# A decoder trunk on one core: the expert rows are put back by two rounded matmuls, and the gate enters at the add

## The chip, the cores and the metric

The kernel runs on one core of a Trainium2 chip. The metric is the device time of one execution in microseconds, here the median of several runs. Five engines matter: TensorE (PE in the rows, with PEld for its weight loads), VectorE (DVE), ScalarE (ACT), GpSimd (POOL) and SyncE (SP), which only starts transfers here. Each engine takes its instructions in order; semaphores order the engines against each other.

## The reference, cut to what matters

The program is a two-layer decoder trunk for 256 tokens of width 1024. The second layer's channel mixer is a mixture of eight experts, each a SwiGLU of width 3584, and every token goes to its best two:

```
top_logit, top_e = lax.top_k(xt @ w_router, 2)
gate = jax.nn.softmax(top_logit, axis=-1)
g, u = jnp.split(xblk @ w_in[e], 2, axis=-1)      # rows of expert e, 128 at a time
yb = (jax.nn.silu(g) * u) @ w_out[e]
out = zeros.at[buf_tok].add(yb * buf_w[:, None])   # buf_w: the gate of each row
h = layer_norm(ALPHA * h + out, ln_g, ln_b)
```

Everything is float32. What this document is about is the line with `add`: the output rows of an expert are multiplied by the gate and added to their tokens.

## The kernel before

The first 554 us or so compute both attention layers, the dense mixer and the router. The rest is a loop of at least eight steps (`steps` is read from the data; it is eight here), one step for each expert, on 128 rows at a time.

Matrix products use *rounded* operands (type float32r, in the names ending in `h` and `l`). A float32 matrix is split in a high part, rounded by ACT, and a low part, the difference, made by DVE. A product is then three rounded matmuls (`product`, L806 to L808): high by high, low by high, high by low. The weights of an expert come as 42 items of 1 MB. For every item SP starts a transfer to one of 11 slots, ACT rounds it into `wh` (L750, 128x2048), DVE writes the difference into `wl` (L1593), and PE does 12 matmuls of 512 columns with it. `wh` and `wl` have three places (`SPLITS`), so ACT may round item k+3 only once PE has used item k (semaphore `used`), DVE follows ACT (`rounded`), and PE follows DVE (`split`). In the body of the loop ACT and DVE run k from 3 to 44, which means that the last three passes (42 to 44) prepare items 0 to 2 of the next expert, and the body begins with item 3.

The order of the other work is written out in a table, `EXPERT_WORK`: before the item k that stands there, ACT and DVE do the activation (`act`), the high and low parts of the turned activation (`turn`), the building of the 0/1 matrices (`build`, `rows`), the taking of the expert's output (`y`, at k = 44, so right before item 2 of the next expert) and the adding back (`back`, at k = 6 and 8).

The rows of one expert go back like this. `put` (128 tokens x 128 slots, twice) holds at [token, slot] the gate if the token has that slot, else 0. PE turns it into `putT`. The output lies in two banks of PSUM, 6 and 7; ACT copies one half into `ysb` (L781) and DVE the other (L1578), both as plain float32. During the next step, after items 3 and 5, PE multiplies `putT` by `ysb` (`scatter`, L1113): four plain float32 matmuls of 512 columns, two after item 3 and two after item 5. DVE adds each result to `pre` (`add_back`, L1550). After the last step four more scatters, the adds and the norm follow, and the output is stored. In the first step `ysb` and `putT` are zeros.

Of the kernel before, what the change touches and what calls it, by code (L numbers as in the profile page):

```python
# [14 lines left out]
P = 128  # L15
# [113 lines left out]
def decoder_kernel(nc, x, positions, w_in_a, w_out_a, cmp_pos, cmp_w1, cmp_w2, w_kv_shared, w_q_b, w_out_b,  # L129
                   sinks_b, ln_g, ln_b, dense_w_in, dense_w_out, moe_router, moe_w_in, moe_w_out, out):  # L130
    ctx = ExitStack()
    with ctx:
# [115 lines left out]
        eactTl = room(3072, 2, 4, P, of=arena_r)  # L248
        act = room(4096, 2, 512)
        esilu = room(5120, 2, 512)  # L250
        ysb = room(6144, D)
        pick = room(7168, NT, P)
        put = room(7424, NT, P)
        putT = room(7680, NT, P)
        slot_at = [ring[:, s, :] for s in range(RING)] + [room(8192, UNIT), room(10240, UNIT), slot9[:, :], slot10[:, :]]

        bank = [ctx.enter_context(nc.psum_tensor(f"bank{i}", [P, 512], F32)) for i in range(8)]
# [65 lines left out]
        e_rows = sem("e_rows")  # L323
        e_rows_high = sem("e_rows_high")
        e_rows_low = sem("e_rows_low")
        e_y_a = sem("e_y_a")
        e_y_v = sem("e_y_v")
        e_back = sem("e_back")
        e_added = sem("e_added")
        done = sem("done")  # L330
# [145 lines left out]
        @block.gpsimd  # L476
        def _(pool):
            n = [0]

            def step(ins):  # L480
                n[0] += 1
                ins.then_inc(consts_step, 1)
                pool.wait_ge(consts_step, n[0])

            step(pool.memset(ident[:, :], 0.0))
            step(pool.affine_select(out=ident[:, :], in_=ident[:, :], compare_op=ALU.not_equal, fill=1.0, base=0,
                                    pattern=[[-1, P]], channel_multiplier=1))
            pool.sem_inc(ident_ready, 1)
            step(pool.tensor_copy(identb[:, :], ident[:, :]))
            for j in range(ROT // 2):  # L490
                step(pool.memset(freq[:, j:j + 1], float(ROPE_THETA ** (-2.0 * j / ROT))))
            step(pool.memset(causal[:, :, :], 0.0))
            step(pool.memset(window[:, :, :], 0.0))
            for m in (causal, window):
                step(pool.affine_select(out=m[:, 1, :], in_=m[:, 1, :], compare_op=ALU.is_ge, fill=NEG, base=0,
                                        pattern=[[-1, P]], channel_multiplier=1))
            step(pool.affine_select(out=window[:, 0, :], in_=window[:, 0, :], compare_op=ALU.is_ge, fill=NEG, base=-1,
                                    pattern=[[1, P]], channel_multiplier=-1))
            step(pool.memset(cmpmask[:, :, :, :], NEG))
            for tt in range(NT):  # L500
                for g in range(4):
                    part = cmpmask[:, tt, g, 16 * g:16 * g + 16]
                    step(pool.memset(part, 0.0))
                    step(pool.affine_select(out=part, in_=part, compare_op=ALU.is_ge, fill=NEG,
                                            base=P * tt - (2 * CMP_STRIDE - 1), pattern=[[-CMP_STRIDE, 16]],
                                            channel_multiplier=1))
            step(pool.memset(seen[:, :], 1.0))
            step(pool.affine_select(out=seen[:, 0:1], in_=seen[:, 0:1], compare_op=ALU.is_ge, fill=0.0,
                                    base=-(2 * CMP_STRIDE - 1), pattern=[[0, 1]], channel_multiplier=1))
            step(pool.memset(onesb[:, :], 1.0))  # L510
            step(pool.affine_select(out=earlier[:, :], in_=onesb[:, :], compare_op=ALU.is_ge, fill=0.0, base=-1,
                                    pattern=[[1, P]], channel_multiplier=-1))
            step(pool.iota(slots[:, :], [[1, P]], base=0, channel_multiplier=0, allow_small_or_imprecise_dtypes=True))
            step(pool.iota(order[:, :, :], [[0, NT], [-1, NE]], base=NE, channel_multiplier=0,
                           allow_small_or_imprecise_dtypes=True))
            step(pool.memset(cmp_in[:, :, :, :], 0.0))
            pool.memset(slotx[:, :, 16:17], -1.0).then_inc(consts, 1)
            pool.memset(gatex[:, :, 16:17], 0.0).then_inc(consts, 1)

            pool.wait_ge(h_ready, 12)  # L520
            pool.tensor_scalar(pre[:, :, :], h[:, :, :], ALPHA, None, ALU.mult).then_inc(e_added, 1)
# [3 lines left out]
        def _(act_e):  # L525
# [225 lines left out]

            norm_part(2, T_H3)
            split_weights(N_FIRST + SPLITS)
            act_e.sem_inc(e_y_a, 1)
            act_e.wait_ge(gap_ready, 1)
            act_e.activation(top[:, 5, :, :], top[:, 4, :, :], ACT.Exp).then_inc(gap_exp, 1)

# [8 lines left out]
            def expert_step(i):  # L766

                for k in range(SPLITS, PER_EXPERT + SPLITS):
                    for what, f in EXPERT_WORK.get(k, ()):
                        if what == "act":  # L770
                            expert_used(act_e, i, EXPERT.index(("g", f, 1)))
                            act_e.wait_ge(e_act, i * FT + max(f - 1, 0) + 1)
                            act_e.activation(esilu[:, f % 2, :], bank[2 * (f % 2)][:, :], ACT.Silu).then_inc(e_silu, 1)
                        elif what == "turn":
                            act_e.wait_ge(e_turned, i * FT + f + 2)
                            act_e.activation(eactTh[:, f % 2, :, :],  # L776
                                             bank[4 + f % 2][:, :].rearrange("p (c n) -> p c n", c=4), ACT.Copy)\
                                 .then_inc(e_high, 1)
                        elif what == "y":
                            expert_used(act_e, i, PER_EXPERT - 1)  # L780
                            act_e.activation(ysb[:, 0:512], bank[6][:, :], ACT.Copy).then_inc(e_y_a, 1)  # L781
                        elif what == "rows":
                            take_rows(i + 2)
                    split_expert(i, k)
# [10 lines left out]
        def _(pe):  # L795
# [307 lines left out]
            def scatter(v, n, last=False):  # L1103

                if n == 0:
                    pe.wait_ge(e_putT_moved, v)
                    pe.wait_ge(e_y_a, v)
                if n == 1:
                    pe.wait_ge(e_y_v, v)
                tt, half = n // 2, n % 2  # L1110
                if n >= 2 and not last:
                    pe.wait_ge(e_added, 4 * v + n - 4)
                pe.matmul(bank[n if last and n >= 2 else 4 + n % 2][:, :], putT[:, tt, :], ysb[:, 512 * half:512 * half + 512],  # L1113
                          start=True, stop=True).then_inc(e_back, 1)


            pe.sem_inc(e_turned, 1)
# [56 lines left out]
        def _(dve):  # L1174
# [354 lines left out]
            step(dve.tensor_tensor(g2, egap, g1, ALU.mult))  # L1529
            step(dve.tensor_tensor(gw, pick1, g1.to_broadcast(wide), ALU.mult))  # L1530
            step(dve.tensor_tensor(tmp, pick2, g2.to_broadcast(wide), ALU.mult))
            dve.tensor_tensor(gatex[:, :, 0:NE], gw, tmp, ALU.add)
            step(dve.tensor_tensor(gatex[:, :, NE:2 * NE], gw, tmp, ALU.add))


            def take_rows(value):
# [3 lines left out]
                    dve.tensor_tensor(xgTl[there], bank[2 + q][:, :].rearrange("p (c n) -> p c n", c=4),  # L1540
                                      xgTh[there].bitcast(F32), ALU.subtract).then_inc(e_rows_low, 1)

            def add_back(v, parts, last=False):

                dve.wait_ge(e_added, 4 * v - 3)
                for n in parts:
                    tt, half = n // 2, n % 2
                    dve.wait_ge(e_back, 4 * v + n - 3)
                    cols = slice(512 * half, 512 * half + 512)
                    dve.tensor_tensor(pre[:, tt, cols], pre[:, tt, cols],  # L1550
                                      bank[n if last and n >= 2 else 4 + n % 2][:, :], ALU.add)\
                       .then_inc(e_added, 1)


            dve.memset(putT, 0.0).then_inc(e_putT_moved, 1)
            dve.memset(ysb, 0.0).then_inc(e_y_v, 1)
            dve.sem_inc(e_act, 1)
            take_rows(1)
            dve.wait_ge(plan_ready, 1)
# [1 line left out]
            with dve.Fori(0, steps) as i:  # L1561
                for k in range(SPLITS, PER_EXPERT + SPLITS):
                    for what, f in EXPERT_WORK.get(k, ()):
# [8 lines left out]
                            dve.tensor_tensor(eactTl[:, f % 2, :, :], bank[4 + f % 2][:, :].rearrange("p (c n) -> p c n", c=4),  # L1572
                                              eactTh[:, f % 2, :, :].bitcast(F32), ALU.subtract).then_inc(e_low, 1)
                        elif what == "back":
                            add_back(i + 1, range(2 * f, 2 * f + 2))
                        elif what == "y":
                            expert_used(dve, i, PER_EXPERT - 1)
                            dve.tensor_copy(ysb[:, 512:1024], bank[7][:, :]).then_inc(e_y_v, 1)  # L1578
                        elif what == "build":
                            build_pick(ds(i + 1, 1), i + 1)  # L1580
                            dve.wait_ge(e_putT, i + 1)
                            for tt in range(NT):
                                ins = dve.tensor_scalar(put[:, tt, :], slots[:, :], slotx[:, tt, ds(i, 1)],
                                                        gatex[:, tt, ds(i, 1)], ALU.is_equal, ALU.mult)
                            ins.then_inc(e_put, 1)
                        else:
                            dve.wait_ge(e_putT, i + 2)
# [8 lines left out]

            dve.wait_ge(ln_landed, 32 * 4)
            for tt in range(NT):
                add_back(steps + 1, range(2 * tt, 2 * tt + 2), last=True)
                dve.wait_ge(e_added, 4 * steps + 3 + 2 * tt)  # L1600
                for half in range(2):
                    chained(dve.bn_stats(stats[:, tt, half, :], pre[:, tt, 512 * half:512 * half + 512]))
                center(tt)
# [25 lines left out]
```

## Time and profile before

| what | value |
|---|---|
| median of 3 runs | 1574.53 us (1573.82 to 1575.28) |
| span of the profiled execution | 1573.7 us, 20472 instructions |
| PE busy | 1512.1 us (96%) |
| DVE busy | 1230.3 us (78%) |
| ACT busy | 982.5 us (62%) |
| POOL busy | 15.2 us (1%) |
| chain that ended last | PE 91%, DVE 5%, ACT 2%, issue 1%, DMA 1% |
| read from memory | 424.14 MB, 270 GB/s over the span |

The profiled execution has no time of its own besides its span; the median of the runs lies 0.8 us above that span. The busy times overlap, so they don't add up. Most of the span belongs to the expert loop, from about 554 us to 1555 us. The last row of the page on the chain says which engine the end of the kernel waited for, step by step, and it counts more than the busy shares.

### The profile page before, as it was taken

How to read it: one execution, taken by the hardware profiler on the slowest of the kernel's cores; microseconds unless marked ns; L12 is line 12 of the kernel's file. 1: busy time of each engine (PE TensorE's matmuls, PEld its weight loads, DVE VectorE, ACT ScalarE, POOL GpSimd, SP SyncE). 2: the span in 40 equal slices, each digit the busy share in tenths (PEclk: the TensorE clock that was granted, in tenths of full speed). 3: DMA queues.
4: the chain of work that ended last, by engine and by line, in shares of the span. 5: the costliest groups of instructions: out<-in, count | busy, mean ns of one | idle time of the engine just before them, and what ended most of it. 6: DMA issues, size and time to landing. Idle time of an engine off the chain costs nothing.

```text
span 1573.7 us, 20472 instructions
## 1 busy us (share of the span) xinstructions
PE 1512.1 (96%) x7467; PEld 1244.6 (79%) x7467; DVE 1230.3 (78%) x1143; ACT 982.5 (62%) x964; POOL 15.2 (1%) x47
## 2 busy tenths in 40 slices
PE   6989989999889799999999999999999999999996
PEld 5876679998776588878888888887887887887884
DVE  5667865454666779889888988988988988988988
ACT  4554534443344367777767777777767777776774
POOL 2000000000000100000000000000000000000000
PEclk9978999999998899999999999999999999999998
DMA  9660026555560489999999999999999999999990
GB/s 333 161 214 1 1 70 199 187 186 188 160 189 1 176 292 346 360 352 334 362 366 356 341 353 354 353 341 359 344 344 367 345 370 334 345 376 347 341 346 27
DMA packets 200922, 425.78 MB, mean 271 GB/s; under 512 B 10384, under 2 KB 42160, under 8 KB 200880
## 3 DMA queue, kind: packets, MB, share of 16 engines
q1 hardware_dynamic: 196864, 419.65, 74.5%
q10 hardware_dynamic: 4016, 5.56, 1.1%
q8 instruction: 27, 0.44, 0.1%
q14 instruction: 15, 0.12, 0.0%
HBM read 424.14 MB, written 1.05 MB: 270 GB/s over the span
## 4 chain that ended last, share of the span: by engine, by line
PE 91%; DVE 5%; ACT 2%; issue 1%; DMA 1%; ACTq 0%; DVEq 0%
PE bank L806 26%; PE bank L808 26%; PE bank L807 26%; PE bank L962 3%; PE bank L823 2%; PE bank L1098 2%; PE bank L1113 2%; PE bank L1159 2%; PE bank L985 1%; PE bank L980 1%; ACT wh L555 1%; DVE wl L1190 1%; DVE h L1435 1%; DVE pre L1426 1%; DVE stats L1419 1%
## 5 line engine op out<-in xcount | busy, mean ns | idle before, releaser
L806 PE MATMUL bank<-wh,arena_r 128*128 128x512 f32 x1432 | 570.5, 398 | 0.0
L1593 DVE TENSOR_TENSOR wl<-ring,wh 128x2048 fp32r<-128x2048 f32 x224 | 512.1, 2291 | 64.9 <-ACT wh L750 64.3
L808 PE MATMUL bank<-wl,arena_r 128*128 128x512 f32 x1432 | 558.5, 390 | 0.0
L807 PE MATMUL bank<-wh,arena_r 128*128 128x512 f32 x1432 | 557.6, 389 | 0.0
L750 ACT ACTIVATE wh<-ring 128x2048 fp32r<-128x2048 f32 x224 | 428.8, 1917 | 93.5 <-PE bank L808 93.4
L806 PEld LDWEIGHTS bank<-wh,arena_r 128*128 128x128 f32 x1432 | 268.9, 188 | 59.3 <-issue 3.8
L807 PEld LDWEIGHTS bank<-wh,arena_r 128*128 128x128 f32 x1432 | 269.1, 188 | 57.7 <-issue 3.8
L808 PEld LDWEIGHTS bank<-wl,arena_r 128*128 128x128 f32 x1432 | 268.8, 188 | 57.4
L1190 DVE TENSOR_TENSOR wl<-ring,wh 128x2048 fp32r<-128x2048 f32 (+1 forms) x64 | 144.7, 2264 | 112.6 <-ACT wh L555 112.6
L555 ACT ACTIVATE wh<-ring 128x2048 fp32r<-128x2048 f32 (+1 forms) x64 | 120.8, 1893 | 128.8 <-PE bank L808 124.4
L1593 DVE TENSOR_TENSOR wl<-arena,wh 128x2048 fp32r<-128x2048 f32 x64 | 146.7, 2292 | 27.7 <-ACT wh L750 27.7
L750 ACT ACTIVATE wh<-arena 128x2048 fp32r<-128x2048 f32 x64 | 122.7, 1917 | 48.8 <-PE bank L808 48.8
L1593 DVE TENSOR_TENSOR wl<-slot,wh 128x2048 fp32r<-128x2048 f32 x48 | 110.0, 2291 | 37.7 <-ACT wh L750 37.7
L750 ACT ACTIVATE wh<-slot 128x2048 fp32r<-128x2048 f32 x48 | 92.1, 1918 | 53.2 <-PE bank L808 53.2
L806 PE MATMUL bank<-hTh,wh 128*128 128x256 f32 x352 | 100.4, 285 | 1.4 <-DVE hTl L1202 1.4
L807 PE MATMUL bank<-hTh,wl 128*128 128x256 f32 x352 | 100.3, 285 | 0.0
L808 PE MATMUL bank<-hTl,wh 128*128 128x256 f32 x352 | 100.2, 285 | 0.0
L806 PE MATMUL bank<-wh,hTh 128*128 128x512 f32 (+2 forms) x208 | 82.6, 397 | 8.3 <-DVE wl L1190 6.5
L689 ACT ACTIVATE arena<-bank,nb 128x128 f32<-128x128 f32 (+1 forms) x128 | 50.7, 406 | 61.4 <-DVE nb L1379 43.7
L808 PE MATMUL bank<-wl,hTh 128*128 128x512 f32 (+2 forms) x208 | 80.0, 385 | 0.0
L807 PE MATMUL bank<-wh,hTl 128*128 128x512 f32 (+2 forms) x208 | 80.0, 385 | 0.0
L776 ACT ACTIVATE arena_r<-bank 128x512 fp32r<-128x512 f32 x56 | 33.5, 599 | 61.8 <-PE bank L1159 61.8
(214 smaller groups left out, 1403.4 us busy)
## 6 DMA issues: line engine op xcount, KB each, us to landing
ring<-in_moe_w_in_dram SPq DMA_DIRECT2D x171, 1024.0 KB
ring<-in_moe_w_out_dram SPq DMA_DIRECT2D x56, 1024.0 KB
arena<-in_moe_w_out_dram SPq DMA_DIRECT2D x40, 1024.0 KB, 5.5
slot<-in_moe_w_in_dram SPq DMA_DIRECT2D x32, 1024.0 KB, 5.0
arena<-in_moe_w_in_dram SPq DMA_DIRECT2D x24, 1024.0 KB, 6.2
ring<-in_dense_w_in_dram SPq DMA_DIRECT2D x22, 1024.0 KB
slot<-in_moe_w_out_dram SPq DMA_DIRECT2D x16, 1024.0 KB, 6.4
ring<-in_dense_w_out_dram SPq DMA_DIRECT2D x11, 1024.0 KB
```

Of the source, the lines that this page charges most:

```text
L555: act_e.activation(wh[:, n % SPLITS, 0:size], slot_of(n)[:, 0:size], ACT.Copy).then_inc(rounded, 1)
L689: ins = act_e.activation(ex[:, i % (lag + 1), k * w:k * w + w], bank[i % 4][:, k * w:k * w + w], ACT.Exp, bias=nb[:, i % 4, k:k + 1], scal ...
L750: act_e.activation(wh[:, n % SPLITS, :], slot_at[SLOT[k % PER_EXPERT]], ACT.Copy).then_inc(rounded, 1)
L776: act_e.activation(eactTh[:, f % 2, :, :], bank[4 + f % 2][:, :].rearrange("p (c n) -> p c n", c=4), ACT.Copy)\
L806: pe.matmul(out_, lh, rh, start=start, stop=False, skip_group_check=True)
L807: pe.matmul(out_, ll, rh, start=False, stop=False, skip_group_check=True)
L808: return pe.matmul(out_, lh, rl, start=False, stop=stop, skip_group_check=True)
L823: ins = pe.transpose(b[:, at:at + rows], src, ident[0:rows, 0:rows])
L962: ins = pe.matmul(sc[:, k * w:k * w + w], q[half, 4 * pb + h0 + k, tt * P:tt * P + P], keys, start=False, stop=(k == nh - 1), skip_group_c ...
L1098: ins = pe.matmul(bank[2 + c // 4][:, (c % 4) * P:(c % 4) * P + P], h[:, tt, c * P:c * P + P], pick[:, tt, :], start=(tt == 0), stop=(tt = ...
L1190: dve.tensor_tensor(wl[:, n % SPLITS, 0:size], slot_of(n)[:, 0:size], wh[:, n % SPLITS, 0:size].bitcast(F32), ALU.subtract).then_inc(split, 1)
L1593: dve.tensor_tensor(wl[:, n % SPLITS, :], slot_at[SLOT[k % PER_EXPERT]], wh[:, n % SPLITS, :].bitcast(F32), ALU.subtract).then_inc(split, 1)
```

## The change

The plain float32 scatter becomes two rounded ones. `putT` is now rounded (float32r) and holds only 0 and 1, since `put` is built without the gate; the output of an expert is kept as a high part `yh`, rounded by ACT from both banks, and a low part `yl`, the difference, made by DVE in two halves. Each scatter is `putT` by `yh` plus `putT` by `yl`, into the same bank. The gate is multiplied in by DVE at the add: `scalar_tensor_tensor` computes bank times gate plus `pre` in one instruction, with the gate as one value per token from `gatex`. `gatex` is shifted by one column, because the first adding back (of zeros) has no expert yet. `yl` has no room of its own: its halves lie in `act[:, 1]` and `esilu[:, 1]`, and so ACT waits for the last scatter before it writes `esilu[:, 1]`.

```
-        ysb = room(6144, D)
+        yh = room(6144, D, of=arena_r)
+        yl = [room(at, 512, of=arena_r) for at in (4096 + 512, 5120 + 512)]
-        putT = room(7680, NT, P)
+        putT = room(7680, NT, P, of=arena_r)
...
                         if what == "act":
                             expert_used(act_e, i, EXPERT.index(("g", f, 1)))
+                            if f == 1:
+                                act_e.wait_ge(e_back, 4 * i + 4)
...
-                            act_e.activation(ysb[:, 0:512], bank[6][:, :], ACT.Copy).then_inc(e_y_a, 1)
+                            for half in range(2):
+                                act_e.activation(yh[:, 512 * half:512 * half + 512], bank[6 + half][:, :], ACT.Copy)\
+                                     .then_inc(e_y_high, 1)
...
                 if n == 0:
                     pe.wait_ge(e_putT_moved, v)
-                    pe.wait_ge(e_y_a, v)
-                if n == 1:
-                    pe.wait_ge(e_y_v, v)
+                if n < 2:
+                    pe.wait_ge(e_y_low, 2 * v + n - 1)
...
-                pe.matmul(bank[n if last and n >= 2 else 4 + n % 2][:, :], putT[:, tt, :], ysb[:, 512 * half:512 * half + 512],
-                          start=True, stop=True).then_inc(e_back, 1)
+                there = bank[n if last and n >= 2 else 4 + n % 2][:, :]
+                pe.matmul(there, putT[:, tt, :], yh[:, 512 * half:512 * half + 512], start=True, stop=False)
+                pe.matmul(there, putT[:, tt, :], yl[half], start=False, stop=True).then_inc(e_back, 1)
...
-                    dve.tensor_tensor(pre[:, tt, cols], pre[:, tt, cols],
-                                      bank[n if last and n >= 2 else 4 + n % 2][:, :], ALU.add)\
-                       .then_inc(e_added, 1)
-            dve.memset(putT, 0.0).then_inc(e_putT_moved, 1)
-            dve.memset(ysb, 0.0).then_inc(e_y_v, 1)
+                    dve.scalar_tensor_tensor(out=pre[:, tt, cols], in0=bank[n if last and n >= 2 else 4 + n % 2][:, :],
+                                             scalar=gatex[:, tt, ds(turn, 1)], in1=pre[:, tt, cols],
+                                             op0=ALU.mult, op1=ALU.add).then_inc(e_added, 1)
+            dve.memset(putT.bitcast(F32), 0.0).then_inc(e_putT_moved, 1)
+            dve.memset(yh.bitcast(F32), 0.0)
+            for half in range(2):
+                dve.memset(yl[half].bitcast(F32), 0.0).then_inc(e_y_low, 1)
...
-                            dve.tensor_copy(ysb[:, 512:1024], bank[7][:, :]).then_inc(e_y_v, 1)
+                            for half in range(2):
+                                dve.wait_ge(e_y_high, 2 * i + half + 1)
+                                dve.tensor_tensor(yl[half], bank[6 + half][:, :],
+                                                  yh[:, 512 * half:512 * half + 512].bitcast(F32), ALU.subtract)\
+                                   .then_inc(e_y_low, 1)
...
                                 ins = dve.tensor_scalar(put[:, tt, :], slots[:, :], slotx[:, tt, ds(i, 1)],
-                                                        gatex[:, tt, ds(i, 1)], ALU.is_equal, ALU.mult)
+                                                        None, ALU.is_equal)
```

ACT at the end of the loop body, where the expert's output is taken; the row before `COMPARE_AND_BRANCH` and its register row is item 2 of the next expert. Before the change:

```order
L781 ACTIVATE arena_61<-bank6 128x512
L394 REGISTER_ALU
L750 ACTIVATE wh_50<-ring_49 128x2048
L789 REGISTER_ALU
L789 COMPARE_AND_BRANCH
```

and after it:

```order
L784 ACTIVATE arena_r_62<-bank6 128x512
L784 ACTIVATE arena_r_62<-bank7 128x512
L395 REGISTER_ALU
L751 ACTIVATE wh_50<-ring_49 128x2048
L793 REGISTER_ALU
L793 COMPARE_AND_BRANCH
```

ACT now has two copies out of the banks ahead of item 2, where it had one.

DVE at the same place, first before the change and then after it (`wl` is the low part of an item, `bank6` and `bank7` hold the expert's output):

```order
L1578 COPY arena_61<-bank7 128x512
L1592 REGISTER_ALU
L1593 TENSOR_TENSOR wl_51<-ring_49,wh_50 128x2048
```

```order
L1585 ISA
L1586 TENSOR_TENSOR arena_r_62<-bank6,arena_r_62 128x512
L1585 REGISTER_ALU
L1586 TENSOR_TENSOR arena_r_62<-bank7,arena_r_62 128x512
L1602 REGISTER_ALU
L1603 TENSOR_TENSOR wl_51<-ring_49,wh_50 128x2048
```

One copy has become two subtractions, still ahead of item 2's low part.

## Rows read from the trace of the kernel before

**Rows 1.** Busy time by stretch: us, PE, PEld, DVE, ACT, POOL, PEclk, DMA, GB/s

```profile
543.00:678.90 135.90, 130.86 (x614) 108.37 (x615) 113.26 (x102) 90.53 (x62) 0.00 (x0) 0.97 0.91 330
678.90:804.10 125.20, 125.20 (x576) 102.59 (x575) 109.28 (x69) 91.39 (x61) 0.00 (x0) 1.00 0.96 352
```

**Rows 2.** Waits of the loop, 553.7 to 1555 us: total, times, longest

```profile
PEld bank L806 <- DVE wl L1593: 2.2, 7, 0.3
```

**Rows 3.** Waits of SP's queue in the loop, from 560 us

```profile
SPq L457 <- DVE wl L1593: 787.6, 318, 15.7
```

**Rows 4.** The chain that ended last, around one scatter: start, us, what

```profile
690.09 1.72 PE bank L1113 x4
691.80 0.23 PE bank L806
692.03 0.23 PE bank L807
```

**Rows 5.** Groups by line, shapes apart: busy us, mean ns, idle before

```profile
L806 PE MATMUL bank<-wh,arena_r 128*128 128x512 f32 x1432 | 570.5, 398 | 0.0
L1113 PE MATMUL bank<-arena 128*128 128x512 f32 x72 | 34.0, 594 | 1.1 <-ACT arena L781 0.8 <-DVE arena L1578 0.3
L1550 DVE TENSOR_TENSOR pre<-pre,bank 128x512 f32<-128x512 f32 x36 | 23.0, 679 | 0.0
L1435 DVE SCALAR_TENSOR_TENSOR h<-pre,std,lnp 128x512 f32<-128x512 f32 x16 | 11.3, 750 | 0.3
```

**Rows 6.** PE's timeline after the turn of an expert: start, us, what

```profile
686.75 0.39 PE L808 MATMUL bank<-wl,arena_r 128*128 128x512 f32 x1
687.03 0.50 PE L806 MATMUL bank<-wh,arena_r 128*128 128x512 f32 x1
687.37 0.40 PE L807 MATMUL bank<-wh,arena_r 128*128 128x512 f32 x1
...
689.70 0.39 PE L808 MATMUL bank<-wl,arena_r 128*128 128x512 f32 x1
...
691.87 0.40 PE L807 MATMUL bank<-wh,arena_r 128*128 128x512 f32 x1
```

**Rows 7.** ACT's timeline at the turn of an expert

```profile
679.02 0.60 ACT L781 ACTIVATE arena<-bank 128x512 f32<-128x512 f32 x1 [0.80 <-PE bank L808]
679.51 1.91 ACT L750 ACTIVATE wh<-ring 128x2048 fp32r<-128x2048 f32 x1
681.44 1.28 ACT L750 ACT_TABLE_LOAD   x1
682.73 3.72 ACT L750 ACTIVATE wh<-ring 128x2048 fp32r<-128x2048 f32 x2
```

**Rows 8.** DVE's timeline at the turn of an expert

```profile
680.46 0.68 DVE L1578 COPY arena<-bank 128x512 f32<-128x512 f32 x1
681.45 2.29 DVE L1593 TENSOR_TENSOR wl<-ring,wh 128x2048 fp32r<-128x2048 f32 x1 [0.31 <-ACT wh L750]
684.68 6.74 DVE L1593 TENSOR_TENSOR wl<-ring,wh 128x2048 fp32r<-128x2048 f32 x3 [0.94 <-ACT wh L750]
...
693.13 2.28 DVE L1593 TENSOR_TENSOR wl<-ring,wh 128x2048 fp32r<-128x2048 f32 x1
```

**Rows 9.** Timeline of all engines after the last expert

```profile
1555.20 0.60 ACT L781 ACTIVATE arena<-bank 128x512 f32<-128x512 f32 x1 [0.80 <-PE bank L808]
1555.70 1.90 ACT L750 ACTIVATE wh<-ring 128x2048 fp32r<-128x2048 f32 x1
...
1557.38 2.84 PE L1113 MATMUL bank<-arena 128*128 128x512 f32 x6 [0.34 <-DVE arena L1578]
...
1557.63 2.29 DVE L1593 TENSOR_TENSOR wl<-ring,wh 128x2048 fp32r<-128x2048 f32 x1 [0.30 <-ACT wh L750]
...
1559.84 1.28 DVE L1550 TENSOR_TENSOR pre<-pre,bank 128x512 f32<-128x512 f32 x2
```

**Rows 10.** Timeline of all engines ahead of the first expert

```profile
550.97 0.91 DVE L1556 MEMSET arena<- 128x1024 f32 x1 [0.16 <-issue]
...
552.83 0.69 DVE L1540 TENSOR_TENSOR arena_r<-bank,arena_r 128x512 fp32r<-128x512 f32 x1 [0.94 <-ACT arena_r L762]
...
553.75 0.49 PE L806 MATMUL bank<-wh,arena_r 128*128 128x512 f32 x1
```

More of the change, by code:

```diff
@@ L325, in decoder_kernel @@
         e_rows_low = sem("e_rows_low")
-        e_y_a = sem("e_y_a")
-        e_y_v = sem("e_y_v")
+        e_y_high = sem("e_y_high")
+        e_y_low = sem("e_y_low")
         e_back = sem("e_back")
@@ L517, in _ @@
             pool.memset(slotx[:, :, 16:17], -1.0).then_inc(consts, 1)
-            pool.memset(gatex[:, :, 16:17], 0.0).then_inc(consts, 1)
+            pool.memset(gatex[:, :, 0:1], 0.0).then_inc(consts, 1)
             pool.wait_ge(h_ready, 12)
@@ L753, in _ @@
             split_weights(N_FIRST + SPLITS)
-            act_e.sem_inc(e_y_a, 1)
             act_e.wait_ge(gap_ready, 1)
@@ L1531, in _ @@
             step(dve.tensor_tensor(tmp, pick2, g2.to_broadcast(wide), ALU.mult))
-            dve.tensor_tensor(gatex[:, :, 0:NE], gw, tmp, ALU.add)
-            step(dve.tensor_tensor(gatex[:, :, NE:2 * NE], gw, tmp, ALU.add))
+            dve.tensor_tensor(gatex[:, :, 1:1 + NE], gw, tmp, ALU.add)
+            step(dve.tensor_tensor(gatex[:, :, 1 + NE:1 + 2 * NE], gw, tmp, ALU.add))
             def take_rows(value):
@@ L1541, in take_rows, with add_back @@
                                       xgTh[there].bitcast(F32), ALU.subtract).then_inc(e_rows_low, 1)
-            def add_back(v, parts, last=False):
+            def add_back(v, turn, parts, last=False):
                 dve.wait_ge(e_added, 4 * v - 3)
@@ L1574, in _ @@
                         elif what == "back":
-                            add_back(i + 1, range(2 * f, 2 * f + 2))
+                            add_back(i + 1, i, range(2 * f, 2 * f + 2))
                         elif what == "y":
                             expert_used(dve, i, PER_EXPERT - 1)
-                            dve.tensor_copy(ysb[:, 512:1024], bank[7][:, :]).then_inc(e_y_v, 1)
+                            for half in range(2):
[3 more added lines that the diff above has]
+                                   .then_inc(e_y_low, 1)
                         elif what == "build":
@@ L1598, in _ @@
             for tt in range(NT):
-                add_back(steps + 1, range(2 * tt, 2 * tt + 2), last=True)
+                add_back(steps + 1, steps, range(2 * tt, 2 * tt + 2), last=True)
                 dve.wait_ge(e_added, 4 * steps + 3 + 2 * tt)
```

## The prediction

> **What bounds the kernel now.** I read the busy times by stretch first, since the shares of the whole span mix stages. One step of the expert loop takes 125.20 us, PE is busy for all of it, DVE for 109.28 us and ACT for 91.39 us [rows 1]. The waits of the loop say the same: PE waits seven times for a low part of the weights, 2.2 us in all, once at each turn from one expert to the next [rows 2]. The loads are not the bound, although the DMA engines are busy for 0.96 of a step: their queue stands 787.6 us waiting for free slots, and slots are freed by DVE [rows 3]. So in the loop the end is set by PE's own work, and DVE and ACT feed it with a few microseconds to spare, least at the turn of an expert. Last come the timelines of PE, ACT and DVE around one turn [rows 6 to 8]; the reader should see who is late there.
>
> **The scatter (gain).** A plain float32 matmul leaves two records: 72 records for 36 matmuls [rows 5]. The recorded length, 594 ns, is not what PE pays, because records overlap. In the chain a pair of scatters (four records) takes 1.72 us, so one scatter 0.86 us, while a rounded matmul of the same shape takes one place of 0.23 us [rows 4]. The pair becomes four rounded matmuls of 128x128 by 512 columns, the form of L806, which stands 1432 times in the trace: 4 x 0.23 = 0.92 us. The gain is 0.80 us a pair. The starts agree: from the L808 ahead of the pair to the second matmul behind it are 691.87 - 689.70 = 2.17 us [rows 6]; six places of 0.23 are 1.38, and the gain is 0.79. There are 16 pairs in the loop (two in each of eight steps, the zeros of the first step included), all where PE bounds: 16 x 0.80 = 12.8 us. The other four scatters stand after the loop and are looked at below.
>
> On this price the trace and the Trainium skill don't quite agree. In the trace a plain float32 scatter costs 0.86 us against 0.23 us for a rounded one, 3.8 places [rows 4]. The Trainium skill, FP8 and Floating Point Precision, section "TensorE Precision Notes", says that true FP32 takes four passes through the array. By that rule, with each pass at the 0.23 us of a rounded matmul, a pair would cost 1.84 us and its replacement 0.92, which makes 16 x 0.92 = 14.7 us instead of 12.8, and the time 1.9 us lower; I go by the row.
>
> **ACT at the turn (loss).** ACT copies bank 6 at 679.02, rounds item 2 from 679.51, loads a table, and rounds item 3 from 682.73 [rows 7]. These follow each other without a gap, so ACT itself is what is late. DVE's low part of item 3 starts at 684.68, right when ACT is done (it sat idle for 0.94 us before that), and takes about 2.29 us [rows 8], and PE's item 3 starts at 687.03, where it should have followed the L808 at 686.75 by 0.23 [rows 6]. So PE is already late there by this chain, and what is put into it shows in full. The change puts a second copy of 128x512 ahead of item 2. Two ACT instructions of this kind follow each other by 0.49 us (679.02 to 679.51) [rows 7]. Item 3 is ready 0.49 us later at each of the 7 turns inside the loop: 3.4 us. Item 2 moves as well: its low part starts at 681.94 instead of 681.45 [rows 8] and ends at 684.23. PE begins item 2 at 686.75 - 11 x 0.227 = 684.26 (twelve matmuls, the last at 686.75), so this is just in time or 0.1 us late; such a slip is contained in the 0.49, since PE waits for item 3 anyway.
>
> Is DVE in time for this? It takes the low halves at 680.46 and about 681.1, each 0.68 us as the copy does, and ACT's copies land at 679.6 and 680.1. DVE is free at 681.7, before the 681.94 at which ACT hands over item 2. So the second subtraction is covered by the wait for ACT (0.31 us before item 2 plus the 0.49 added) [rows 8]. Without that cover it would cost 0.6 us a turn. PE's wait for `yl` is over at 681.8, eight microseconds ahead of the scatter.
>
> **Items 4 to 8 (nothing).** The shorter pairs take 0.8 us of time away from ACT and DVE, twice. DVE makes the low parts of items 3 to 5 one behind the other, 2.2 us apart [rows 8]; PE starts item 3 at 687.52 and takes 2.8 us for an item and 0.92 for a pair. So the low part of item 4 ends at 689.7 against 691.2 when PE wants it, item 5 at 691.9 against 693.9, item 6, behind the activation and two adds, at about 696.0 (before: 693.13 + 2.28 = 695.4 [rows 8]) against 697.6. The spare time is 1.5 us or more at each, so no new wait.
>
> **The add (nothing in the loop).** The form with a scalar per token takes 750 ns where both tensors are in SBUF, the plain add 679 ns [rows 5]; the new one lies between 0 and 0.07 us above the old. In the loop DVE has 16 us a step to spare [rows 1]. I take 0.07.
>
> **The tail (loss).** After the last expert the four scatters are not what is waited for: PE begins the last three at 1557.38 and is done with them well before DVE, which first makes a low part that nobody needs (1557.63, when ACT hands it over) and adds from 1559.84 [rows 9]. ACT's extra 0.49 us moves that hand-over; the scatters' gain is worth nothing here. Four adds on the way to the end cost up to 4 x 0.07 = 0.3 us. Loss: 0.8 us.
>
> **The rest (nothing).** The zeroing grows by two halves of 512 columns, about as much as the 0.91 us of the present 1024 [rows 10]. The DVE instruction behind it starts at 552.83 after 0.94 us of idling, and PE starts at 553.75: nothing, at most 0.1 us. ACT's new wait before `esilu[:, 1]` stands two items behind item 8, the last scatter ahead of item 6: it is over before. Building `put` without the gate saves DVE a little where it has room.
>
> **The sum.** 12.8 - 3.4 - 0.8 = 8.6 us. Against the profiled span, 1573.7 - 8.6 = 1565.1 us. The median of the runs lies 0.8 us above that span, so I forecast 1565.9 us.
>
> **Rivals.**
> *The turn hides the copy.* If ACT's table load or the item behind it absorbs the second copy (a shorter gap between copies, or DVE catching up), 0 instead of 3.4 us is lost: 12.0 us gained, 1562.5 us; with the price of the four passes 1560.6 us. Against it: ACT shows no gap between 679.02 and the end of item 4 [rows 7]. Chance 0.14.
> *The feed becomes the bound behind the scatters.* Were item 6 or 7 late, the second pair's 0.80 us would be lost in eight steps: 6.4 us less, 1572.3 us. For it speaks that everything hangs on three places of `wh`; against it the spare 1.5 us. Chance 0.08, with the smaller losses between.
> *Slower: the rounded scatter is not cheap.* It would be so if the matmul on `putT`, written by DVE's copy, ran at the pace of the plain form, or if two matmuls that accumulate into one bank cost more than two apart. The change costs 3.4 + 0.8 = 4.2 us elsewhere, 0.26 us a pair; from (1.72 - 0.26) / 4 = 0.365 us for each rounded matmul on, the kernel is slower. At 0.43 (a record of the plain form) it is 1574.5 + 4.2 = 1578.7 us. The 1432 matmuls at 0.23 [rows 4, 5] speak against it. Chance 0.03.
> *PE's granted clock falls.* It is 1.00 in the loop and 0.97 in the stretch that holds the loop's start [rows 1]. At 0.99 a thousand microseconds of loop grow by 10 us and the gain is gone. PE is busy all the time before and after, so I give it 0.02.
>
> **How the numbers follow.** The forecast itself, 1563.5 to 1568.5, has 0.73. The range for 8 in 10 reaches to the first rival and a little into the second: 1562.0 to 1569.5. A measurement of this kernel can tell 0.2%, 3.1 us, from no change. Faster by more than that: the forecast, the first rival and a part of the second, 0.91. Within: most of the rest of the second, 0.05. Slower: the last two, 0.04.
>
> **What would show it.** Four records for a pair of scatters at starts 0.23 us apart; a step between experts of about 124.1 us (125.2 - 1.6 + 0.5); two ACT copies 0.49 us apart ahead of item 2; PE's wait for item 3 grown from 0.3 to about 0.7 us, still 7 times, perhaps with 0.1 us at item 2; no wait at items 4 to 8; in the tail a first add of DVE that comes 0.5 us later after the last expert than now. The prediction is wrong if the pair takes over 1.2 us, if PE waits in other places, or if the wait at item 3 doesn't grow.

## The result and the profile after

The kernel after takes 1564.32 us (median of 4 runs, 1563.51 to 1565.67) against 1574.9 us for the kernel before (median of 4, 1573.82 to 1576.22). The ratio is 0.9933 with a 95% interval of 0.9918 to 0.9947, so 8 to 13 us faster. The forecast was 1565.9 us, range 1562.0 to 1569.5. The profiled execution of the kernel after has a span of 1563.0 us against 1573.7 us, 10.7 us less, where 8.6 us were forecast. The 0.8 us that the forecast put between that span and the median is not a fixed distance: every execution whose own span is on record takes 1.67 to 2.26 us more than it, and the median of this kernel lies 1.3 us above the profiled span.

First the scatter. PE's timeline after the turn of an expert, as in [rows 6] of the kernel before (start, us, engine, line, what); line 812 is the last of the three matmuls of a product, L810 and L811 are the first two:

```profile
681.24 0.39 PE L812 MATMUL bank<-wl,arena_r 128*128 128x512 f32 x1
681.50 0.50 PE L810 MATMUL bank<-wh,arena_r 128*128 128x512 f32 x1
681.84 0.40 PE L811 MATMUL bank<-wh,arena_r 128*128 128x512 f32 x1
...
684.17 0.39 PE L812 MATMUL bank<-wl,arena_r 128*128 128x512 f32 x1
684.73 0.50 PE L810 MATMUL bank<-wh,arena_r 128*128 128x512 f32 x1 [0.17 <-DVE wl L1603]
685.07 0.40 PE L811 MATMUL bank<-wh,arena_r 128*128 128x512 f32 x1
...
687.39 0.39 PE L812 MATMUL bank<-wl,arena_r 128*128 128x512 f32 x1
687.62 0.39 PE L1117 MATMUL bank<-arena_r 128*128 128x512 f32 x1
687.85 0.39 PE L1118 MATMUL bank<-arena_r 128*128 128x512 f32 x1
688.07 0.39 PE L1117 MATMUL bank<-arena_r 128*128 128x512 f32 x1
688.30 0.39 PE L1118 MATMUL bank<-arena_r 128*128 128x512 f32 x1
688.53 0.39 PE L810 MATMUL bank<-wh,arena_r 128*128 128x512 f32 x1
688.75 0.39 PE L811 MATMUL bank<-wh,arena_r 128*128 128x512 f32 x1
```

The four rounded matmuls stand 0.23 us apart, in step with the products around them. From the last matmul ahead of the pair to the second behind it are 688.75 - 687.39 = 1.36 us, where [rows 6] have 2.17: 0.81 us less. Item 2 begins at 681.50, 0.03 us late against the pace of 0.23. Item 3 begins at 684.73, where it should have followed the L812 at 684.17 by 0.23: 0.33 us lost, and in the kernel before it was 0.05.

Then the turn. ACT, and below it DVE, as in [rows 7, 8]:

```profile
676.23 1.09 ACT L784 ACTIVATE arena_r<-bank 128x512 fp32r<-128x512 f32 x2 [0.80 <-PE bank L812]
677.20 1.92 ACT L751 ACTIVATE wh<-ring 128x2048 fp32r<-128x2048 f32 x1
679.14 1.28 ACT L751 ACT_TABLE_LOAD   x1
680.43 3.72 ACT L751 ACTIVATE wh<-ring 128x2048 fp32r<-128x2048 f32 x2
```

```profile
677.67 1.28 DVE L1586 TENSOR_TENSOR arena_r<-bank,arena_r 128x512 fp32r<-128x512 f32 x2
679.15 2.29 DVE L1603 TENSOR_TENSOR wl<-ring,wh 128x2048 fp32r<-128x2048 f32 x1 [0.20 <-ACT wh L751]
682.38 6.69 DVE L1603 TENSOR_TENSOR wl<-ring,wh 128x2048 fp32r<-128x2048 f32 x3 [0.94 <-ACT wh L751]
```

From ACT's first copy to its rounding of item 3 are now 4.20 us, before 3.71 [rows 7]. From the same copy to PE's item 3 are now 684.73 - 676.23 = 8.50 us, before 687.03 - 679.02 = 8.01 [rows 6, 7]. DVE is ready at 678.9 and still waits 0.20 us for ACT. In PE's waits of the loop (total, times, longest) there are now 14 where [rows 2] had 7, in two entries, since a wait can be seen at the weight load or at the matmul:

```profile
PEld bank L810 <- DVE wl L1603: 6.2, 14, 0.6
...
PE bank L810 <- DVE wl L1603: 1.2, 7, 0.2
```

Seven of the 14 are at item 2 and seven at item 3, one of each at every turn; the longest, at item 3, has grown from 0.3 to 0.6 us. None is at items 4 to 8.

The add, and the stretch of one step, as in [rows 5] and [rows 1]:

```profile
L1554 DVE SCALAR_TENSOR_TENSOR pre<-bank,gatex,pre 128x512 f32<-128x512 f32 x36 | 25.2, 742 | 0.0
```

```profile
677.30:801.30 124.00, 123.83 (x576) 102.55 (x575) 109.98 (x70) 91.95 (x64) 0.00 (x0) 1.00 0.98 355
```

The granted clock (third number from the right) stays at 1.00 of 2.4 GHz, as in [rows 1], and over the whole loop, 552.6 to 1543.8 us, it is 1.00 too: the rival of the falling clock is out.

**The account.** ACT's table load at the top of the loop's body marks each step. The marks of the kernel before stand 125.17 us apart, those of the kernel after 123.93 us. With the starts of the first matmul of the loop (before at 553.75 us, after at 552.67 us) and of the last one, the span divides in three:

| stretch | before, us | after, us | difference | forecast |
|---|---|---|---|---|
| up to the loop's first matmul | 553.75 | 552.67 | -1.08 | 0 |
| loop, first to last matmul | 1001.03 | 990.68 | -10.35 | -9.4 |
| last matmul to the end | 18.92 | 19.65 | +0.73 | +0.8 |

### The profile page after: what moved, and what is told of

Read it like the earlier page. It is cut to its first block, busy times and chain, and to the rows that moved or that the text cites. A ratio compares the mean times of both kernels' runs of the same rounds, so it can differ in the third digit from the quotient of the medians.

```text
span 1563.0 us, 20531 instructions
## 1 busy us (share of the span) xinstructions
PE 1497.8 (96%) x7467; PEld 1242.9 (80%) x7467; DVE 1236.7 (79%) x1153; ACT 986.6 (63%) x972; POOL 15.2 (1%) x47
## 4 chain that ended last, share of the span: by engine, by line
PE 87%; DVE 6%; ACT 4%; issue 1%; DMA 1%; ACTq 0%; DVEq 0%
PE bank L810 25%; PE bank L812 25%; PE bank L811 25%; PE bank L966 3%; PE bank L827 2%; PE bank L1102 2%; ACT wh L751 2%; PE bank L1163 2%; PE bank L989 1%; DVE wl L1603 1%; PE bank L984 1%; ACT wh L556 1%; DVE wl L1194 1%; DVE h L1439 1%; ACT L751 1%
## 5 line engine op out<-in xcount | busy, mean ns | idle before, releaser
L810 PE MATMUL bank<-wh,arena_r 128*128 128x512 f32 x1432 | 564.7, 394 | 1.2 <-DVE wl L1603 1.2
L812 PE MATMUL bank<-wl,arena_r 128*128 128x512 f32 x1432 | 558.2, 390 | 0.0
L811 PE MATMUL bank<-wh,arena_r 128*128 128x512 f32 x1432 | 557.8, 390 | 0.0
L810 PEld LDWEIGHTS bank<-wh,arena_r 128*128 128x128 f32 x1432 | 268.9, 188 | 60.1 <-DVE wl L1603 6.2
L812 PEld LDWEIGHTS bank<-wl,arena_r 128*128 128x128 f32 x1432 | 268.8, 188 | 57.2
L811 PEld LDWEIGHTS bank<-wh,arena_r 128*128 128x128 f32 x1432 | 269.1, 188 | 53.8
L810 PE MATMUL bank<-hTh,wh 128*128 128x256 f32 x352 | 100.4, 285 | 1.4 <-DVE hTl L1206 1.4
L811 PE MATMUL bank<-hTh,wl 128*128 128x256 f32 x352 | 100.2, 285 | 0.0
L812 PE MATMUL bank<-hTl,wh 128*128 128x256 f32 x352 | 100.1, 285 | 0.0
L810 PE MATMUL bank<-wh,hTh 128*128 128x512 f32 (+2 forms) x208 | 82.2, 395 | 8.4 <-DVE wl L1194 6.6
L812 PE MATMUL bank<-wl,hTh 128*128 128x512 f32 (+2 forms) x208 | 79.8, 384 | 0.0
L811 PE MATMUL bank<-wh,hTl 128*128 128x512 f32 (+2 forms) x208 | 79.8, 384 | 0.0
```

Of the source, the lines that this page charges most:

```text
L810: pe.matmul(out_, lh, rh, start=start, stop=False, skip_group_check=True)
L811: pe.matmul(out_, ll, rh, start=False, stop=False, skip_group_check=True)
L812: return pe.matmul(out_, lh, rl, start=False, stop=stop, skip_group_check=True)
```

## The experiments

Each kernel starts from the kernel after. The column "step" is the distance of two marks, "loop" runs from the first to the last matmul, "tail" from there to the end, all from one profiled execution; the median is of several runs. The ratio is to a set of runs of the kernel before from the same session: the set of 1574.9 us for the kernel after, 1574.15 us for e1 to e4, 1575.31 us for e5 and e6.

| kernel | median, us | ratio (95%) | step | loop | tail | loop starts |
|---|---|---|---|---|---|---|
| before | 1574.9, 1574.15 and 1575.31 (three sets) | 1 | 125.17 | 1001.03 | 18.92 | 553.75 |
| after | 1564.32 | 0.9933 (0.9918 to 0.9947) | 123.93 | 990.68 | 19.65 | 552.67 |
| e1_plain_scatter | 1578.08 | 1.0025 (1.0016 to 1.0035) | 125.62 | 1004.15 | 19.71 | 552.94 |
| e2_high_only | 1557.45 | 0.9893 (0.9877 to 0.991) | 122.99 | 983.16 | 19.63 | 554.11 |
| e3_three_copies | 1568.07 | 0.9965 (0.9952 to 0.9977) | 124.43 | 994.16 | 20.18 | 551.26 |
| e4_dve_rounds_half | 1562.6 | 0.9928 (0.9911 to 0.9944) | 123.73 | 989.26 | 19.99 | 554.05 |
| e5_plain_add | 1564.57 | 0.9933 (0.9918 to 0.9949) | 123.93 | 990.67 | 19.40 | 553.03 |
| e6_y_later | 1560.8 | 0.9915 (0.9901 to 0.9928) | 123.24 | 985.81 | 20.74 | 551.35 |

**e1_plain_scatter: the scatter's price alone.**

```
-                pe.matmul(there, putT[:, tt, :], yh[:, 512 * half:512 * half + 512], start=True, stop=False)
-                pe.matmul(there, putT[:, tt, :], yl[half], start=False, stop=True).then_inc(e_back, 1)
+                pe.matmul(there, putT[:, tt, :].bitcast(F32), yh[:, 512 * half:512 * half + 512].bitcast(F32),
+                          start=True, stop=True).then_inc(e_back, 1)
```

> The kernel after, with the scatter as one plain float32 matmul again (on yh; the low part of the rows is left out). Everything else stays: two ACT copies, two DVE subtractions, the gate at the add. Theory (a plain pair costs its 1.72 us and besides slows the rounded matmuls behind it): a step between experts goes from 123.94 to 125.65 us, 0.855 us a pair, the whole about 13.7 us slower than the kernel after, near 1578. Rival (the pair costs 0.80 us more and no more; the 2 us gained beyond the forecast came from somewhere else): a step of 125.54 us, and the rounded matmuls behind the pair stand 0.227 us apart. Rival by the four passes: 0.92 us a pair, a step of 125.78 us.

Measured: a step of 125.62 us, 1.69 more than the kernel after, 0.845 us a pair; the loop is 13.47 us longer, 16 x 0.84. That is between the forecast's 0.80 and the 0.855 of the first theory, nearer to the latter. The Trainium skill, FP8 and Floating Point Precision, section "TensorE Precision Notes", says that true FP32 takes four passes through the array; with each pass at 0.23 us, a pair is estimated at 0.92 us more than its replacement, and the measurement is below that. The part above 0.80 can be seen behind the pair. PE's timeline of this kernel:

```profile
689.36 0.39 PE L812 MATMUL bank<-wl,arena_r 128*128 128x512 f32 x1
689.58 1.88 PE L1117 MATMUL bank<-arena_r 128*128 128x512 f32 x4
690.90 0.79 PE L810 MATMUL bank<-wh,arena_r 128*128 128x512 f32 x1
691.53 0.40 PE L811 MATMUL bank<-wh,arena_r 128*128 128x512 f32 x1
...
693.84 0.39 PE L812 MATMUL bank<-wl,arena_r 128*128 128x512 f32 x1
```

and of the kernel after, the same ten places on:

```profile
691.02 0.39 PE L812 MATMUL bank<-wl,arena_r 128*128 128x512 f32 x1
```

From the second matmul behind the pair to the twelfth are 693.84 - 691.53 = 2.31 us here and 691.02 - 688.75 = 2.27 us in the kernel after: 0.231 against 0.227 us a place. So a plain float32 pair costs 1.72 us itself and leaves the rounded matmuls behind it slower for some ten places, 0.04 us in all. But it is not the plain form alone that does this. In the kernel after, with rounded matmuls on both sides of the wait at item 3, the second to the twelfth matmul (685.07 to 687.39, in the timeline above) also take 2.32 us for ten places, and in the kernel before 689.70 - 687.37 = 2.33 [rows 6]; behind the turning of an activation (four matmuls of 128x128) the ten places take 2.31 us (700.99 to 703.30 in the kernel after). Behind the rounded scatters they take 2.27. What the slow stretches have in common is a break in the stream of rounded matmuls. Why a break has this effect is open.

The experiment also gives the price of everything else in the change: e1 has the old scatter's pace and the new turn, and its step is 125.62 - 125.17 = 0.45 us longer than the step before.

**e2_high_only: is PE the bound behind the scatters?**

```
-                pe.matmul(there, putT[:, tt, :], yh[:, 512 * half:512 * half + 512], start=True, stop=False)
-                pe.matmul(there, putT[:, tt, :], yl[half], start=False, stop=True).then_inc(e_back, 1)
+                pe.matmul(there, putT[:, tt, :], yh[:, 512 * half:512 * half + 512], start=True, stop=True)\
+                  .then_inc(e_back, 1)
```

> The kernel after, with the scatter by the high part alone: one rounded matmul where there are two (the low part is made by DVE and not used). Theory (PE sets the pace behind the turn, every matmul is a place of 0.227 us): a step falls by 4 x 0.227 = 0.91 us to 123.03 us, the whole by 7.3 us to about 1557. Rival (ACT and DVE have become the bound behind the scatters): a step falls by less than 0.5 us and new waits of PE for the low parts stand at items 4 to 8.

Measured: the step is 0.94 us shorter (122.99), the median 1557.45 us, the loop 7.5 us shorter, and PE's waits for low parts are those of the kernel after (6.3 us, 14 times, and 1.3 us, 7 times). ACT and DVE would have followed a still shorter scatter. The rival of a feed that becomes the bound behind the scatters is refuted, with at least 0.9 us a step to spare beyond what the change takes.

**e3_three_copies: is ACT what is late at the turn?**

```
                                 act_e.activation(yh[:, 512 * half:512 * half + 512], bank[6 + half][:, :], ACT.Copy)\
                                      .then_inc(e_y_high, 1)
+                            act_e.activation(esilu[:, 0, :], esilu[:, 0, :], ACT.Copy)
```

> The kernel after, with a third ACT copy of 128x512 (within SBUF, of nothing that is needed) behind the two at the turn of an expert. Theory (ACT is what is late at the turn, an added copy shows in full): PE's item 3 starts 0.5 us later at each of the 7 turns and the tail grows by 0.5 us: a step of 124.43 us, the whole 4 us slower than the kernel after, about 1568.3. Rival (the copy is hidden; the turn cost something else): no change, 1564.3.

Measured: a step of 124.43 us, 0.50 more; the tail 0.53 us longer; the median 1568.07 us. The added copy shows in full at each turn. PE's waits of the loop, as above:

```profile
PEld bank L811 <- DVE wl L1604: 10.1, 14, 0.8
...
PE bank L811 <- DVE wl L1604: 4.2, 14, 0.4
```

**e4_dve_rounds_half: could DVE take the second copy?**

```
-                            for half in range(2):
-                                act_e.activation(yh[:, 512 * half:512 * half + 512], bank[6 + half][:, :], ACT.Copy)\
-                                     .then_inc(e_y_high, 1)
+                            act_e.activation(yh[:, 0:512], bank[6][:, :], ACT.Copy).then_inc(e_y_high, 1)
...
+                            dve.tensor_copy(yh[:, 512:1024], bank[7][:, :]).then_inc(e_y_half, 1)
                             for half in range(2):
-                                dve.wait_ge(e_y_high, 2 * i + half + 1)
+                                dve.wait_ge((e_y_high, e_y_half)[half], i + 1)
```

> The kernel after, with the high part of the second half made by DVE, so that ACT has one copy at the turn as in the kernel before, and DVE three instructions. Theory (ACT and DVE are both out of time at the turn; DVE is free 0.3 us late for item 2 when it has 0.6 us more): item 3 doesn't wait any more, but item 2 does by about 0.3 us, PE restarts there, and the step stays within 0.2 us of 123.94; the whole 1564 to 1565. Rival (ACT alone limits the turn): 0.49 us less a step, 123.45 us, the whole about 1560.5.

Measured: a step of 123.73 us, 0.20 less than the kernel after, and a tail 0.34 us longer; the median of 1562.6 us can't be told from the kernel after. DVE at the turn:

```profile
679.05 0.68 DVE L1583 CAST arena_r<-bank 128x512 fp32r<-128x512 f32 x1
679.65 1.28 DVE L1586 TENSOR_TENSOR arena_r<-bank,arena_r 128x512 fp32r<-128x512 f32 x2
680.85 6.92 DVE L1603 TENSOR_TENSOR wl<-ring,wh 128x2048 fp32r<-128x2048 f32 x3
```

DVE doesn't idle any more: item 2's low part starts when DVE is free, and not when ACT is done, and item 3's follows at once. PE waits 7 times instead of 14, now at item 2. So the turn has a second limit right behind the first, and the copy costs nearly as much on DVE.

**e5_plain_add: the gate at the add.**

```
-                    dve.scalar_tensor_tensor(out=pre[:, tt, cols], in0=bank[n if last and n >= 2 else 4 + n % 2][:, :],
-                                             scalar=gatex[:, tt, ds(turn, 1)], in1=pre[:, tt, cols],
-                                             op0=ALU.mult, op1=ALU.add).then_inc(e_added, 1)
+                    dve.tensor_tensor(pre[:, tt, cols], pre[:, tt, cols],
+                                      bank[n if last and n >= 2 else 4 + n % 2][:, :], ALU.add)\
+                       .then_inc(e_added, 1)
...
-                                                        None, ALU.is_equal)
+                                                        gatex[:, tt, ds(i + 1, 1)], ALU.is_equal, ALU.mult)
```

> The kernel after, with the gate in the 0/1 matrix as before the change and a plain add (the gate is then rounded with the matrix). Theory (the slower form of the add shows in the tail alone): a step as in the kernel after, 123.94 us; in the tail four adds shorter by 0.06 us, 0.25 us in all, so 1564.1, which the runs can't tell from 1564.3. Rival (DVE's time counts in the loop too): 36 x 0.062 = 2.2 us less, 1562.1, and a shorter step.

Measured: the add takes 682 ns instead of 741 (medians), the step stays at 123.93 us, the loop is the same to 0.01 us, and the tail is 0.25 us shorter. So the fused add costs nothing in the loop and 0.25 us at the end, as the theory says; the medians of the runs (1564.57 and 1564.32 us) don't tell such a size.

**e6_y_later: take the output off the turn.**

```
-EXPERT_WORK = {PER_EXPERT + SPLITS - 1: [("y", 0)]}
+EXPERT_WORK = {4: [("y", 0)]}
...
             with act_e.Fori(0, steps) as i:
                 expert_step(i)
+            take_y()
             norm_part(3, None)
...
+            take_y(steps)
             dve.wait_ge(ln_landed, 32 * 4)
             for tt in range(NT):
                 add_back(steps + 1, steps, range(2 * tt, 2 * tt + 2), last=True)
```

`take_y` holds the two copies of ACT, or the two subtractions of DVE. It no longer waits for `used`, since ACT's rounding of item 3 has waited for a later item already, and the zeroing of `yh` and `yl` is gone.

> The kernel after, with the taking of the expert's output (two ACT copies, two DVE subtractions) moved from before item 2 of the next expert to before item 4, behind ACT's table load and item 3; the last expert's output is taken after the loop. Theory (what PE loses at the turn is ACT's time between the last matmul of an expert and the rounding of item 3): PE no longer waits at items 2 and 3, 0.64 us less a step, 123.30 us; the output is ready at about 1.2 us ahead of the scatter; the tail grows by 0.9 us since the item that nobody needs is then split first: the whole 7 x 0.64 - 0.9 = 3.6 us less, 1560.7. Rival (the copies cost as much wherever they stand, since ACT and DVE have no room before item 4 either): PE waits at item 4 or 6, and the whole is not faster than 1564.

Measured: a step of 123.24 us, 0.69 less than the kernel after, a tail 1.09 us longer, a median of 1560.8 us. ACT, DVE and the whole step:

```profile
676.85 1.28 ACT L751 ACT_TABLE_LOAD   x1
678.14 1.92 ACT L751 ACTIVATE wh<-ring 128x2048 fp32r<-128x2048 f32 x1
679.97 1.06 ACT L768 ACTIVATE arena_r<-bank 128x512 fp32r<-128x512 f32 x2
680.92 1.92 ACT L751 ACTIVATE wh<-ring 128x2048 fp32r<-128x2048 f32 x1
```

```profile
682.30 1.28 DVE L1553 TENSOR_TENSOR arena_r<-bank,arena_r 128x512 fp32r<-128x512 f32 x2
683.50 4.49 DVE L1605 TENSOR_TENSOR wl<-ring,wh 128x2048 fp32r<-128x2048 f32 x2
```

```profile
676.85:800.09 123.24, 123.24 (x576) 102.68 (x575) 109.77 (x69) 91.90 (x63) 0.00 (x0) 1.00 0.98 357
```

The list of waits of this loop has no entry of PE at all, and PE is busy for the whole step. The same two copies and two subtractions are free two items later. This is the fastest of the kernels that use both parts of the output (e2 is faster, but leaves the low part out): 0.9915 of the kernel before. Against the kernel after, by the profiles, it wins 4.87 us in the loop and gives back 1.09 us in the tail. There DVE first makes the low part that nobody needs and then takes the output:

```profile
1539.53 2.29 DVE L1605 TENSOR_TENSOR wl<-ring,wh 128x2048 fp32r<-128x2048 f32 x1 [0.41 <-ACT wh L751]
...
1541.74 1.28 DVE L1553 TENSOR_TENSOR arena_r<-bank,arena_r 128x512 fp32r<-128x512 f32 x2
1542.48 0.59 PE L1120 MATMUL bank<-arena_r 128*128 128x512 f32 x1 [4.93 <-DVE arena_r L1553]
```

## Why the prediction was right, and where its sizes were off

**What bounds (right).** PE's own work and, at the turn, ACT ahead of it. e2 shows the first (matmuls left out shorten the step by their full price), e3 the second (a copy put in lengthens it by its full price), e6 both: with nothing at the turn PE is busy for 123.24 of 123.24 us.

**The scatter (right, the term too small).** Forecast 0.80 us a pair, 12.8 in all; e1 measures 0.845 and 13.5. The 0.80 was the pair itself; missing was what the plain form does to the matmuls behind it, 0.04 us a pair. No row of the prediction was wrong here, its stretch was too short: the 0.04 could have been had from the kernel before by measuring from the last matmul ahead of the pair to the twelfth behind it instead of to the second. The measurement lies between this 0.80 and the 0.92 a pair, 14.7 in all, that the prediction gives as its second price. That second price is the estimate from the Trainium skill, FP8 and Floating Point Precision, section "TensorE Precision Notes".

**The turn (right, a little too large).** Forecast 0.49 us at 7 turns, 3.4 us; e1 against the kernel before gives 0.45 us, 3.1 us. The 0.49 of ACT's copy arrives in full at item 3, as ACT's 4.20 us against 3.71 and PE's 8.50 us against 8.01 say. But PE's loss isn't one wait that grows. There are two: the slip at item 2 that the prediction allowed for is there at each turn (item 2 starts at 681.50, where DVE has made its low part just then), and the wait at item 3 follows. So of the signs that the prediction names, the wait is there 14 times and not 7. The missing 0.04 us of a step is not at item 3; it is spread over the rest of the step, too thin for rows of 0.01 us to place it. With e6 as the zero, the turn costs PE 0.69 us in the kernel after and 125.17 - 1.69 - 123.24 = 0.24 us in the kernel before.

The rows of PE add up to nearly the same, if each break is charged with the time lost, the slow start (0.34 - 0.23 = 0.11 us) and the ten slower places (0.05 to 0.06 us). Before: 0.05 + 0.11 + 0.06 = 0.22 us. After: 0.03 + 0.11 + 0.06 = 0.20 us at item 2 and 0.33 + 0.11 + 0.05 = 0.49 us at item 3, together 0.69.

**DVE at the turn (right).** The second subtraction was hidden by the wait for ACT, and 0.20 us of that wait are left; the prediction had 0.2 (681.7 against 681.94). e4 shows how thin this cover is.

**Items 4 to 8, the add in the loop, the start (right).** No new wait; the add cost nothing (e5). The two zeroings ahead of the loop ended inside DVE's idle time.

**The tail (right).** Forecast +0.8, measured +0.73: ACT's copy 0.49 and the four adds 0.25 (e5). DVE's first add now starts 5.55 us after the start of the loop's last matmul (1548.90 and 1543.35), before 5.06 (1559.84 [rows 9] and 1554.78).

**The 1.08 us ahead of the loop** are most likely not of the change, though no experiment isolates them. That part of the program has nearly the same work in all eight kernels: only the zeroing just before the loop and the column in which the gates lie differ. Yet in their profiles the loop starts anywhere from 551.26 to 554.11 us, with e3 (the zeroings as in the kernel after) earliest and e2 (the same zeroings) latest. One profile of each kernel can't tell 1 us there. The granted clock of the first 200 us goes along with it, though this is no proof of a cause: 0.93 and 0.85 in its two halves in the kernel before, e2 and e4, which start the loop at 553.75 to 554.11, 0.97 to 0.98 and 0.85 to 0.86 in the kernel after, e1 and e5 (552.67 to 553.03), 0.95 and 0.88 in e3 and e6 (551.26 and 551.35). So part of how well the total of a single profile fits a forecast is luck. Loop and tail alone give -9.6 us against the 8.6 forecast, and the forecast's terms account for the rest: +0.7 from the pairs, +0.3 from the turns.

**The rivals.** That the turn hides the copy: refuted by e3. That the feed becomes the bound: refuted by e2. That the rounded scatter is not cheap: refuted by its 0.23 us. That the clock falls: refuted by its 1.00.

## What to carry to other kernels

Where PE is busy all the time, price a matmul by the distance of starts and not by its recorded length, and measure across the ten or so matmuls behind it: a plain float32 matmul of 512 columns costs 0.86 us against 0.23 for a rounded one, so two rounded ones, by the high and by the low part, are a gain even if the preparation grows. Two are enough here because the other operand holds only 0 and 1 and needs no low part; this is why the gate had to leave the matrix. Then look at where the preparation stands: the same two copies and two subtractions cost 0.69 us a step right before item 2, ahead of the table load at the head of the loop's body, and nothing two items later (e6). An engine that is busy for 74% of a step can still be what the step waits for, at one place of it.

## What the runs showed of the hardware that was not expected

Rounded matmuls run slower for a while behind a break in their stream. The first one takes longer to the next start, and the ten places behind it take 2.31 to 2.33 us instead of 2.27. This is so behind a pair of plain float32 matmuls (e1 and the kernel before), behind the four turning matmuls of 128x128, and behind a wait with rounded matmuls on both sides (kernel after, 684.73 and on). It is not so behind a pair of rounded scatters (kernel after, 688.53 and on). After a wait the first matmul takes 0.34 us to the next start instead of 0.23 (684.73 to 685.07). So a wait costs about 0.16 us more than the time for which PE stands: 0.11 at the first matmul and 0.05 over the next ten places. That is why a turn at which the kernel before loses 0.05 us to waiting costs it 0.24 us with e6 as the zero.
